# Expert weight chunks fetched as two 1 MB transfers instead of one of 2 MB

## The chip, the cores and the metric

The kernel runs on one core of one Trainium2 chip. The metric is the time of one execution on the device in microseconds (us). TensorE (PE) does the matrix products, VectorE (DVE), ScalarE (ACT) and GpSimd (POOL) do the rest, and SyncE (SP) issues all DMA transfers.

## The reference

One inference step of a two-layer backbone for 128 prompt tokens and 256 sample tokens, all in float32, with a model width of 1024. Each layer has four parallel token mixers with gates (half one) and then an expert-choice feed-forward stage (half two). The change touches the second half:

```python
def expert_choice_ffn(h, w_router, w_gate, w_up, w_down):
    B, L, D = h.shape
    cap = EC_CAPACITY * L // N_EXPERTS          # 16 prompt, 32 sample tokens per expert
    aff = jax.nn.softmax((h @ w_router).astype(jnp.float32), axis=-1)
    g, idx = lax.top_k(jnp.swapaxes(aff, 1, 2), cap)
    xs = jax.vmap(lambda hb, ib: hb[ib])(h, idx)
    a = jnp.einsum('becd,edf->becf', xs, w_gate)
    u = jnp.einsum('becd,edf->becf', xs, w_up)
    y = jnp.einsum('becf,efd->becd', jax.nn.silu(a) * u, w_down) * g[..., None].astype(h.dtype)
    return jax.vmap(lambda ib, yb: jnp.zeros((L, D), yb.dtype).at[ib.reshape(-1)].add(yb.reshape(-1, D)))(idx, y)
```

There are 16 experts. Each has three 1024x1024 float32 matrices (gate, up, down), 12 MB, so that a layer's experts are 192 MB (201 million bytes) which are read once.

## The kernel before, in words

**Chunks.** An expert's weights lie in memory as six chunks of 2 MB: four (PAIRS = 4) of gate and up, each for two of the eight blocks k of the contraction, and two of down, each for four blocks k. A chunk is 128 rows, one for a partition, of 16 KB: four sub-rows of 1024 words. A gate/up block k needs two sub-rows (gate, up), a down block k one. PER = 6 chunks make an expert and 96 make a layer; below they are counted as x = 0 to 95.

**The ring.** Eight places hold chunks (RING = 8, order in PLACE): six are slots of the array `ring`, one is `high_slot`, and one is made of two pieces, `low_slot` for three sub-rows and a stretch of the constants' array C for the fourth (place 7, with x = 1, 9, 17, ...). `fetch` issues a chunk as one DMA (lines 565, 566 and 568: place 7 takes two, of 1.5 and 0.5 MB), all from SP on one queue. `chunk_landed` is PE's wait on the semaphore e_land of the place.

**Order on SP.** `mixer_sync` issues x = 0 to 6 before the expert stage, as places come free from the mixers' use of the same memory; its first four go out early, x = 4 to 6 when the output projection has ended. `experts_sync` issues x = 7, and then waits for each chunk n to be used up (`used_chunk`) before it issues x = n + 8 into its place. Chunk use is told by PE: e_pair after the second block k of the first three gate/up chunks, the closing of the product's PSUM bank after the fourth, e_down_half after k = 3 of down, and the closing of y after k = 7. After the last chunk SP issues the next layer's small parameters (line 747), the four modulation chunks ada0 to ada3 (line 727) and the first input weights in two transfers of 1 MB (line 733, rows of 8 KB).

**Order on PE.** `experts_tensor` loops over groups of four experts. For each it does `gate_up` (line 1702, with the gathers of line 1670 between the blocks of the first expert of a group), then `down`: transposes (lines 1716 and 1719) and products (line 1731). In the trace a float32 product counts as two MATMUL records. A group ends with idle products (line 692) and the combination (line 1748). After the last group of layer 0 PE goes on to the opening of layer 1 (lines 698, 635, 638 and 639); line 900, DVE's line 1367 and line 934 then begin its mixers.

```python
if k % 2 == 0:
    chunk_landed(pe, g, j * PER + k // 2)
...
if k % 2 and k < KT - 1:
    ins.then_inc(S["e_pair"], 1)
```

Of the kernel before, what the change touches and what calls it, by code (L numbers as in the profile page):

```python
# [29 lines left out]
D = 1024  # L30
KT = D // P
# [108 lines left out]
def build(nc, A):  # L140
    ctx = ExitStack()
    with ctx:
# [5 lines left out]
        def sem(name):  # L148
            s = ctx.enter_context(nc.semaphore(name))
            sems.append(s)  # L150
            return s
# [69 lines left out]
        def adas(c):  # L221
# [94 lines left out]
        names = ("x_mixed b_high b_rest br_high br_rest rest_in grow_in sink_in cache_in nab_in nab_ready u_zero "  # L316
                 "sc_ready dve_step route_step conv_step rope_ready scores_done scores_read nmax_ready exps_done p_ready "
                 "pv0 pv1 high_act rest_pool high_dve rest_dve w_high w_rest mask_in dft_in gate_add out_kv n2_sq n2_ms n2_sd n2_rs n2_xn wr_in wrm_ready router_max router_exp wk_prompt aff_ready affg_ready "
                 "cum_ready sel_ready selg_ready e_pair e_down_half silu_done x_done prompt_part").split() + list(OPENING)
        land = [sem(f"land{s}") for s in range(NSLOT)]  # L320
        e_land = [sem(f"e_land{s}") for s in range(8)]
        full = [sem(f"full{b}") for b in range(8)]
        free = [sem(f"free{b}") for b in range(8)]
        e_full = [sem(f"e_full{b}") for b in range(8)]
# [5 lines left out]
            scores_read=6, nmax_ready=6, exps_done=7, p_ready=6, pv0=6, pv1=6, high_act=4, rest_pool=4, high_dve=4,  # L330
            rest_dve=4, w_high=48, w_rest=48, mask_in=16, dft_in=16, gate_add=24, out_kv=64, n2_sq=4, n2_ms=3, n2_sd=3,
            n2_rs=3, n2_xn=3, wr_in=16, wrm_ready=2, router_max=1, router_exp=1, wk_prompt=2, aff_ready=1, affg_ready=1,
            cum_ready=1, sel_ready=5, selg_ready=5, e_pair=48, e_down_half=16, silu_done=32, x_done=12, prompt_part=8, op_full=3, op_free=2,
            op_prm=1, op_mod=2, op_gain=1, op_sq=3, op_sd=3, op_rs=3, op_xn=3)
        assert set(PER_LAYER) == set(names)

# [137 lines left out]
        def layer(l):  # L474
# [77 lines left out]
            PER = PAIRS + 2  # L552
            PLACE = (4, 7, 6, 5, 1, 2, 0, 3)
            RING = len(PLACE)

            def chunk(l, e, i):

                name, part = ("w_e_gu", i) if i < PAIRS else ("w_e_down", i - PAIRS)
                return A[name][bass.ds(l, 1), bass.ds(e, 1), part].rearrange("o e p n -> p (o e n)")

            def fetch(sp, x, src):

                s, landing = PLACE[x % RING], e_land[x % RING]
                if s == 7:
                    sp.dma_start(low_slot, src[:, 0:3 * D]).then_inc(landing, 16)
                    sp.dma_start(C[:, FIRST:FIRST + D], src[:, 3 * D:4 * D]).then_inc(landing, 16)
                else:
                    sp.dma_start(high_slot if s == 6 else ring[:, s, :], src).then_inc(landing, 16)

            def chunk_row(x, r):  # L570

# [2 lines left out]
                    return low_slot[:, r * D:(r + 1) * D] if r < 3 else C[:, FIRST:FIRST + D]  # L574
                return (high_slot if s == 6 else ring[:, s, :])[:, r * D:(r + 1) * D]

            def chunk_landed(pe, g, x):

                n = 32 if PLACE[x % RING] == 7 else 16
                pe.wait_ge(e_land[x % RING], n * (l * NE * PER // RING + x // RING + 1) + g * (n * GRP * PER // RING))  # L580


            E = BankTurns()
# [203 lines left out]
            def mixer_sync(sp):  # L787
# [50 lines left out]

                for x in range(RING - 1):
                    s = PLACE[x]  # L840
                    if s < 4:
                        used_up(sp, latest[s])
                    elif s == 4:
                        copied(sp, f"o{len(ATT) - 1}")
                    elif s == 5:
                        take(sp, f"p{GATE_ORDER[-1]}_{KT - 1}")
                    elif s == 6:
                        sp.wait_ge(S["gate_add"], base("gate_add") + 3 * KT)
                    elif s == 7:
                        take(sp, parts[-1][0])  # L850
                    fetch(sp, x, chunk(l, x // PER, x % PER))

            def mixer_gpsimd(pool):
                pool.wait_ge(S["op_full"], base("op_full") + 1)
# [740 lines left out]


            def experts_sync(sp):
                def used_chunk(g, j, i):

                    if i < PAIRS - 1:  # L1600
                        sp.wait_ge(S["e_pair"], base("e_pair") + (PAIRS - 1) * (GRP * g + j) + i + 1)
                    elif i == PAIRS - 1:
                        e_take(sp, g, f"gu{j}_1")
                    elif i == PAIRS:
                        sp.wait_ge(S["e_down_half"], base("e_down_half") + GRP * g + j + 1)
                    else:
                        e_take(sp, g, f"y{j}")

                if l > DEPTH - 2:
                    sp.wait_ge(S["x_mixed"], base("x_mixed") + 2 * TT)  # L1610
                    sp.dma_start(GROW[:, 0, 0, :], A["final_norm_g"].rearrange("(o d) -> o d", o=1).broadcast_to((P, D))).then_inc(
                        once["fin_g_in"], 16)
                used_up(sp, "ada11")
                fetch(sp, RING - 1, chunk(l, (RING - 1) // PER, (RING - 1) % PER))
                with sp.Fori(0, NE // GRP - 1) as g:
                    for n in range(GRP * PER):
                        used_chunk(g, n // PER, n % PER)
                        x = n + RING
                        fetch(sp, x, chunk(l, g * GRP + x // PER, x % PER))
                last = NE // GRP - 1  # L1620
                for n in range(GRP * PER - RING):
                    used_chunk(last, n // PER, n % PER)
                    x = n + RING
                    fetch(sp, x, chunk(l, last * GRP + x // PER, x % PER))

                if l < DEPTH - 1:
                    load_parameters(sp, l + 1)
                    for name in ("ada0", "ada2", "ada1", "ada3", "w0"):
                        n = GRP * PER - RING + PLACE.index(unit_at[name][0])
                        used_chunk(last, n // PER, n % PER)  # L1630
                        if name == "w0":
                            load_first_weights(sp, l + 1)
                        else:
                            load_ada(sp, l + 1, int(name[3:]))

                if l > DEPTH - 2:
                    for i, t in enumerate(ROWS):
                        dst = A["y_prompt"] if t == 0 else A["y_sample"][:, (t - 1) * P:t * P]
                        sp.wait_ge(once["fin_y"], i + 1)
                        sp.dma_start(dst.rearrange("b s d -> (b s) d"), XN[:, t, :]).then_inc(once["fin_out"], 16)  # L1640
                    sp.wait_ge(once["fin_out"], TT * 16)

            def experts_tensor(pe):
# [20 lines left out]
                with pe.Fori(0, NE // GRP) as g:  # L1664
# [21 lines left out]
                    def gate_up(j):  # L1686

                        pb = [e_open(pe, g, f"gu{j}_{half}") for half in range(2)]
                        for k, halves in [(k, (0, 1)) for k in range(KT - 2)] + [(k, (half,)) for half in range(2) for k in (KT - 2, KT - 1)]:
                            if j == 0 and 0 in halves and 0 < k < KT - 1:  # L1690
                                for ahead in ((k + 1,) if k < KT - 3 else (k + 1, k + 2) if k == KT - 3 else ()):
                                    gather(ahead)
                                if k == KT - 2:
                                    affinities_t()
                            if k % 2 == 0:
                                chunk_landed(pe, g, j * PER + k // 2)
                            if j == 0 and 0 in halves:
                                e_copied(pe, g, f"xe{k}")
                            for half in halves:
                                for m in range(2):  # L1700
                                    w = chunk_row(j * PER + k // 2, 2 * (k % 2) + m)
                                    ins = nc.tensor.matmul(pb[half][64 * m:64 * m + 64, :], XE[:, k, j, :],  # L1702
                                                           w[:, half * CH:(half + 1) * CH], start=(k == 0),
                                                           stop=(k == KT - 1))
                                if k == KT - 1:
                                    e_close(ins, f"gu{j}_{half}")
                            if k % 2 and k < KT - 1:
                                ins.then_inc(S["e_pair"], 1)

                    def down(j):  # L1710
                        for k in range(KT):
# [12 lines left out]
                        for k in range(KT):  # L1724
                            if k % 4 == 0:
                                e_copied(pe, g, f"at{j}_{k // 4}")
                            x = j * PER + PAIRS + k // 4
                            if k % 4 == 0:
                                chunk_landed(pe, g, x)
                            for half in range(2):  # L1730
                                ins = nc.tensor.matmul(ps[64 * half:64 * half + 64, :], AT[:, k, :],  # L1731
                                                       chunk_row(x, k % 4)[:, half * CH:(half + 1) * CH],
                                                       start=(k == 0), stop=(k == KT - 1))
                            if k == 3:
                                ins.then_inc(S["e_down_half"], 1)
                        e_close(ins, f"y{j}")

                    for j in range(GRP):
# [277 lines left out]
```

## Time and profile before

| | us |
|---|---|
| three runs | 1712.97, 1716.68, 1717.48; median 1716.68 |
| the profiled execution | 1710.48, with a span of 1708.4 |
| PE busy | 1578.7 (92% of the span) |
| DVE, ACT, POOL busy | 505.0, 489.6, 322.2 |
| q1, SP's DMA queue | 52296 packets, 535.43 MB, 76.4% of 16 engines' span |

The DMA engines are busy in nine tenths and more of every slice from some 430 us to the end of the first expert stage (850 us), and again from some 1260 to 1685 us. In these stretches they move 427 to 429 GB/s. The granted clock of TensorE is at full speed in nearly all slices.

### The profile page before, as it was taken

What the parts mean: (1) busy time and instruction counts of PE and PEld (TensorE: products, weight loads), DVE (VectorE), ACT (ScalarE), POOL (GpSimd) and SP (SyncE); (2) the same over time, 40 slices, a digit from 0 to 9 for tenths busy, and PEclk for the clock granted to TensorE, in tenths of its full rate; (3) what the DMA queues carried; (4) which work ended last, traced back from release to release, by engine and by line L of the source; (5) the groups of instructions that cost most, each with busy time, mean ns of one, the idle gap of its engine ahead of it and who ended that gap; (6) DMA issues with size and microseconds to landing.
All of it is one profiled execution on the core that took longest, in us unless ns stands there. A gap on an engine that the chain in (4) does not pass through costs nothing.

```text
span 1708.4 us, 20755 instructions
## 1 busy us (share of the span) xinstructions
PE 1578.7 (92%) x8277; PEld 936.1 (55%) x8277; DVE 505.0 (30%) x854; ACT 489.6 (29%) x892; POOL 322.2 (19%) x182
## 2 busy tenths in 40 slices
PE   7999999999999899799899999999999998988986
PEld 4988899944333333243269888897533432432422
DVE  3723454423120121121157234533321211112113
ACT  4435454214012121120153455431321211211211
POOL 1544456400000000000035444552000000000000
PEclk9999999999999999999999999999999999999999
DMA  9624433558999999999994433356499999999995
GB/s 382 227 99 157 149 148 148 196 248 322 423 427 427 428 428 427 429 427 427 423 394 155 140 117 148 148 185 251 183 399 428 427 428 427 427 428 427 428 428 244
DMA packets 52357, 536.29 MB, mean 314 GB/s; under 512 B 13616, under 2 KB 14024, under 8 KB 20296
## 3 DMA queue, kind: packets, MB, share of 16 engines
q1 hardware_dynamic: 52296, 535.43, 76.4%
q8 instruction: 43, 0.70, 0.2%
q14 instruction: 18, 0.15, 0.0%
HBM read 533.05 MB, written 2.36 MB: 313 GB/s over the span
## 4 chain that ended last, share of the span: by engine, by line
PE 70%; DMA 21%; DVE 4%; ACT 3%; issue 1%; SPq 0%; POOL 0%; DVEq 0%; ACTq 0%
PE psum L934 22%; PE psum L1702 18%; DMA ring<-in_w_e_down 12%; PE psum L1731 8%; DMA ring<-in_w_e_gu 7%; PE psum L1167 4%; PE psum L1097 3%; PE psum L1670 3%; PE psum L698 2%; PE psum L1748 2%; DMA ring<-in_w_ada 1%; PE psum L692 1%; PE psum L1070 1%; PE psum L1049 1%; ACT WSR L1186 1%
## 5 line engine op out<-in xcount | busy, mean ns | idle before, releaser
L934 PE MATMUL psum<-HTH,WSR 128*128 128x384 f32 x1536 | 411.4, 341 | 4.8 <-DVE HTL L1378 4.2
L1702 PE MATMUL psum<-ring,arena 128*64 128x512 f32 x1536 | 344.7, 596 | 36.5 <-DMA ring<-in_w_e_gu 34.6
L934 PEld LDWEIGHTS psum<-HTH,WSR 128*128 128x128 f32 x1536 | 279.4, 188 | 18.4 <-issue 11.4
L878 POOL TENSOR_TENSOR WSR<-ring,WSR 128x1024 fp32r<-128x1024 f32 x94 | 228.9, 2435 | 255.2 <-ACT WSR L1186 255.2
L934 PE MATMUL psum<-HTL,WSR 128*128 128x384 f32 x768 | 258.7, 337 | 0.0
L1702 PEld LDWEIGHTS psum<-ring,arena 128*64 128x64 f32 x1536 | 105.4, 137 | 255.5 <-issue 189.0
L1879 DVE TENSOR_TENSOR arena<-arena,psum 64x512 f32<-64x512 f32 x64 | 44.1, 690 | 507.4 <-ACT arena L1785 507.4
L1186 ACT ACTIVATE WSR<-ring 128x1024 fp32r<-128x1024 f32 x96 | 101.6, 1058 | 289.1 <-PE psum L934 289.1
L1731 PE MATMUL psum<-ring,arena 128*64 128x512 f32 x768 | 172.8, 596 | 3.7 <-DMA ring<-in_w_e_down 3.7
L934 PEld LDWEIGHTS psum<-HTL,WSR 128*128 128x128 f32 x768 | 144.3, 188 | 1.0 <-issue 1.0
L1785 ACT ACTIVATE arena<-psum 64x512 f32<-64x512 f32 x64 | 37.7, 589 | 347.3 <-PE psum L1702 346.6
L1702 PE MATMUL psum<-arena 128*64 128x512 f32 x448 | 119.8, 599 | 8.0 <-DMA arena<-in_w_e_gu 8.0
L1790 ACT ACTIVATE arena<-psum 32x512 f32<-32x512 f32 x64 | 37.7, 590 | 269.2 <-PE psum L1731 268.8
L1731 PEld LDWEIGHTS psum<-ring,arena 128*64 128x64 f32 x768 | 53.7, 137 | 102.0 <-issue 100.4
L1868 DVE TENSOR_TENSOR arena<-psum,GROW 32x512 f32<-32x512 f32 x64 | 43.8, 684 | 210.4 <-PE psum L1731 210.0
L855 POOL MEMSET arena<- 128x888 f32 x2 | 1.7, 837 | 545.4 <-PE psum L698 545.4
L620 ACT ACTIVATE arena<-psum,MOD,SC 128x128 f32<-128x128 f32 (+1 forms) x144 | 57.2, 460 | 123.2 <-PE psum L1670 118.7
L1167 PE MATMUL psum<-ring,arena 128*128 128x512 f32 x192 | 85.4, 596 | 3.1 <-DMA ring<-in_w_out 1.6
L1468 DVE TENSOR_TENSOR arena<-arena 128x384 f32<-128x384 f32 x48 | 72.2, 1503 | 1.7
L1702 PEld LDWEIGHTS psum<-arena 128*64 128x64 f32 x448 | 34.2, 136 | 67.4 <-issue 63.5
L1670 PEld LDWEIGHTS psum<-arena,XN 128*128 128x128 f32 x384 | 47.0, 191 | 37.5 <-issue 37.5
L1465 DVE TENSOR_TENSOR arena<-arena,psum 128x384 f32<-128x384 f32 x48 | 26.6, 554 | 130.5 <-ACT arena L1279 111.8
(218 smaller groups left out, 1622.8 us busy)
## 6 DMA issues: line engine op xcount, KB each, us to landing
ring<-in_w_e_gu SPq DMA_DIRECT2D x96, 2048.0 KB, 28.1
ring<-in_w_e_down SPq DMA_DIRECT2D x48, 2048.0 KB, 31.0
ring<-in_w_ada SPq DMA_DIRECT2D x24, 2048.0 KB, 9.4
ring<-in_w_in SPq DMA_DIRECT2D x22, 2048.0 KB, 8.2
arena<-in_w_e_gu SPq DMA_DIRECT2D x16, 2048.0 KB, 30.0
arena<-in_w_e_gu SPq DMA_DIRECT2D x16, 1536.0 KB, 23.6
arena<-in_w_e_down SPq DMA_DIRECT2D x8, 2048.0 KB, 23.4
arena<-in_w_e_down SPq DMA_DIRECT2D x8, 1536.0 KB, 28.6
```

The costliest lines, as they stand in the source:

```text
L620: return nc.scalar.activation(dst, src, ACT.Identity, scale=SC[:, which, k, i:i + 1], bias=MOD[:, sec * KT + k, i:i + 1])
L878: nc.gpsimd.tensor_tensor(WSR[:, 1, i % 2], part_src(i), WSR[:, 0, i % 2].bitcast(F32), ALU.subtract).then_inc(S["w_rest"], 1)
L934: ins = nc.tensor.matmul(ps[:, 0:TOK], WSR[:, w, i % 2, k, :], x[:, k, :], start=(k == 0 and w == 0 and x is HTH), stop=(k == KT - 1 and w ...
L1097: ins = nc.tensor.matmul(ps[:, 0:TOK], w[:, idx % 2, c, :], x[:, c, :], start=(ins is None), stop=(c == 1 and w is BWL))
L1167: ins = nc.tensor.matmul(ps[:, :], MRG[:, k, t * P:(t + 1) * P], wo[:, k % 4, half * CH:(half + 1) * CH], start=(k == 0), stop=(k == KT - 1))
L1186: nc.scalar.activation(WSR[:, 0, i % 2], part_src(i), ACT.Copy).then_inc(S["w_high"], 1)
L1468: nc.vector.tensor_tensor(MRG[:, k, :], MRG[:, k, :], GP[:, idx % 2, :], ALU.add).then_inc(S["gate_add"], 1)
L1670: ins = nc.tensor.matmul(ps[:, c0:c0 + P], XN[:, t, k * P:(k + 1) * P], SEL[:, AT_PLACE[t]].rearrange("p e s -> p (e s)"), start=(t != 2), ...
L1702: ins = nc.tensor.matmul(pb[half][64 * m:64 * m + 64, :], XE[:, k, j, :], w[:, half * CH:(half + 1) * CH], start=(k == 0), stop=(k == KT - 1))
L1731: ins = nc.tensor.matmul(ps[64 * half:64 * half + 64, :], AT[:, k, :], chunk_row(x, k % 4)[:, half * CH:(half + 1) * CH], start=(k == 0), ...
L1868: ins = nc.vector.tensor_tensor(YS[rows, cols], ps[64 * half:64 * half + 32, :], GROW[64 * half:64 * half + 32, 1, 1, cols], ALU.mult)
L1879: e_release(nc.vector.tensor_tensor(AA[0:64, cols], TMP[64:128, cols], ps[64:128, :], ALU.mult), f"gu{j}_{half}")
```

## The change

Every chunk goes as two transfers, one of sub-rows 0 and 1 and one of sub-rows 2 and 3; rows of 16 KB in the transfer become rows of 8 KB. Each half has its own landing semaphore (16 in place of 8). PE waits for the half that a block needs, and says that it has used a half; SP waits for a half and then issues the half that takes its memory. Place 7 now takes three transfers: 1 MB, 0.5 MB and 0.5 MB. The number of bytes, the ring, the order of the chunks and PE's products stay as they are.

```diff
-            def fetch(sp, x, src):
-                s, landing = PLACE[x % RING], e_land[x % RING]
-                if s == 7:
-                    sp.dma_start(low_slot, src[:, 0:3 * D]).then_inc(landing, 16)
+            def fetch(sp, x, h, src):
+                s, landing = PLACE[x % RING], e_land[x % RING][h]
+                if s == 7 and h:
+                    sp.dma_start(low_slot[:, 2 * D:3 * D], src[:, 2 * D:3 * D]).then_inc(landing, 16)
                     sp.dma_start(C[:, FIRST:FIRST + D], src[:, 3 * D:4 * D]).then_inc(landing, 16)
                 else:
-                    sp.dma_start(high_slot if s == 6 else ring[:, s, :], src).then_inc(landing, 16)
+                    rows = slice(2 * h * D, 2 * (h + 1) * D)
+                    dst = low_slot if s == 7 else high_slot if s == 6 else ring[:, s, :]
+                    sp.dma_start(dst[:, rows], src[:, rows]).then_inc(landing, 16)
...
-                def used_chunk(g, j, i):
-                    if i < PAIRS - 1:
-                        sp.wait_ge(S["e_pair"], base("e_pair") + (PAIRS - 1) * (GRP * g + j) + i + 1)
-                    elif i == PAIRS - 1:
-                        e_take(sp, g, f"gu{j}_1")
-                    elif i == PAIRS:
-                        sp.wait_ge(S["e_down_half"], base("e_down_half") + GRP * g + j + 1)
+                def used_half(g, j, i, h):
+                    done = base("e_half") + HALVES * (GRP * g + j)
+                    if i < PAIRS:
+                        if (i, h) == (PAIRS - 1, 1):
+                            e_take(sp, g, f"gu{j}_1")
+                        else:
+                            sp.wait_ge(S["e_half"], done + 2 * i + h + 1)
+                    elif (i, h) == (PER - 1, 1):
+                        e_take(sp, g, f"y{j}")
                     else:
-                        e_take(sp, g, f"y{j}")
+                        sp.wait_ge(S["e_half"], done + KT - 1 + 2 * (i - PAIRS) + h + 1)
...
                     for n in range(GRP * PER):
-                        used_chunk(g, n // PER, n % PER)
                         x = n + RING
-                        fetch(sp, x, chunk(l, g * GRP + x // PER, x % PER))
+                        for h in range(2):
+                            used_half(g, n // PER, n % PER, h)
+                            fetch(sp, x, h, chunk(l, g * GRP + x // PER, x % PER))
...
-                            if k % 2 == 0:
-                                chunk_landed(pe, g, j * PER + k // 2)
+                            if k < KT - 2 or 0 in halves:
+                                chunk_landed(pe, g, j * PER + k // 2, k % 2)
...
-                            if k % 2 and k < KT - 1:
-                                ins.then_inc(S["e_pair"], 1)
+                            if k < KT - 1 and 1 in halves:
+                                ins.then_inc(S["e_half"], 1)
...
-                            if k % 4 == 0:
-                                chunk_landed(pe, g, x)
+                            if k % 2 == 0:
+                                chunk_landed(pe, g, x, k % 4 // 2)
...
-                            if k == 3:
-                                ins.then_inc(S["e_down_half"], 1)
+                            if k % 2 and k < KT - 1:
+                                ins.then_inc(S["e_half"], 1)
```

## Rows read from the trace of the kernel before

**Rows 1.** The DMA queues' view of 450 to 845 us: packets, MB, share of 16 engines.
```profile
DMA packets 13038, 168.92 MB, mean 428 GB/s; under 512 B 1448, under 2 KB 1448, under 8 KB 2728
q1 hardware_dynamic: 13036, 168.89, 100.7%
```
**Rows 2.** PE's waits of 1300 to 1700 us: total us, times, longest us.
```profile
PE psum L1702 <- DMA ring<-in_w_e_gu: 17.3, 15, 1.2
PE psum L1702 <- DMA arena<-in_w_e_gu: 4.0, 3, 1.4
```
**Rows 3.** Chain that ended last, its end: start us, us, what.
```profile
1653.13 35.45 DMA ring<-in_w_e_down
1688.59 0.14 issue
1688.72 3.65 PE psum L1731 x16
1692.38 1.49 PE psum L692 x4
```
**Rows 4.** SP's DMA issues at the first stage's start: start us, us of issuing.
```profile
389.88 0.81 SPq L568 DMA_DIRECT2D ring<-in_w_e_down  x2
410.89 0.36 SPq L568 DMA_DIRECT2D ring<-in_w_e_gu  x1
415.95 0.34 SPq L565 DMA_DIRECT2D arena<-in_w_e_gu  x1
422.06 0.33 SPq L568 DMA_DIRECT2D arena<-in_w_e_down  x1
426.13 0.33 SPq L568 DMA_DIRECT2D ring<-in_w_e_down  x1
```
**Rows 5.** The chain of waits in the same stretch: PE's first blocks k.
```profile
405.62 1.94 PE psum L1702 x8
407.55 0.87 PE psum L1670 x6
408.42 1.87 PE psum L1702 x8
```
**Rows 6.** Stretches of 10 us, both stages' starts: busy us (instructions), then clock, DMA share, GB/s.
```profile
410.00:420.00 10.00, 10.00 (x58) 5.16 (x56) 0.00 (x0) 3.04 (x8) 0.00 (x0) 1.00 0.90 338
420.00:430.00 10.00, 9.04 (x48) 3.54 (x49) 1.80 (x3) 4.23 (x8) 0.00 (x0) 1.00 0.98 371
430.00:440.00 10.00, 10.00 (x48) 3.30 (x46) 1.36 (x2) 1.19 (x2) 0.00 (x0) 1.00 0.98 406
1250.00:1260.00 10.00, 10.00 (x58) 5.08 (x58) 0.00 (x0) 3.61 (x10) 0.00 (x0) 1.00 0.98 394
1260.00:1270.00 10.00, 9.05 (x49) 3.40 (x46) 1.80 (x3) 3.66 (x6) 0.00 (x0) 1.00 0.97 363
```
**Rows 7.** DMA queues of 464 to 496 us: rows of 16 KB nearly alone.
```profile
DMA packets 995, 13.78 MB, mean 431 GB/s; under 512 B 109, under 2 KB 109, under 8 KB 169
q1 hardware_dynamic: 994, 13.76, 101.2%
```
**Rows 8.** DMA queues of 866 to 871 us: the first input weights, rows of 8 KB.
```profile
DMA packets 247, 2.05 MB, mean 410 GB/s; under 512 B 30, under 2 KB 30, under 8 KB 30
q1 hardware_dynamic: 247, 2.05, 97.7%
```
**Rows 9.** SP's issues before the first stage ends.
```profile
815.39 16.09 SPq L747 DMA_DIRECT2D arena<-in_conv_ln_g  x1
842.67 2.36 SPq L727 DMA_DIRECT2D ring<-in_w_ada  x1
```
**Rows 10.** Line 727's last issue, 842 to 846 us: time from issue to landing.
```profile
DMA to landing us min/median/max: 26.6/26.6/26.6
```
**Rows 11.** The chain of waits at the first stage's end.
```profile
849.33 3.65 PE psum L1731 x16
867.78 4.85 PE psum L698 x32
872.63 1.88 PE psum L900 x16
```
**Rows 12.** PE's weight loads of line 698, in order of time.
```profile
868.63 0.20 PEld L698 LDWEIGHTS psum<-ring,condT 128*32 128x32 f32 x4 [0.65 <-issue]
870.31 0.12 PEld L698 LDWEIGHTS psum<-ring,condT 128*32 128x32 f32 x4 [0.63 <-issue]
```

More of the change, by code:

```diff
@@ L318, in build @@
                  "pv0 pv1 high_act rest_pool high_dve rest_dve w_high w_rest mask_in dft_in gate_add out_kv n2_sq n2_ms n2_sd n2_rs n2_xn wr_in wrm_ready router_max router_exp wk_prompt aff_ready affg_ready "
-                 "cum_ready sel_ready selg_ready e_pair e_down_half silu_done x_done prompt_part").split() + list(OPENING)
+                 "cum_ready sel_ready selg_ready e_half silu_done x_done prompt_part").split() + list(OPENING)
         land = [sem(f"land{s}") for s in range(NSLOT)]
-        e_land = [sem(f"e_land{s}") for s in range(8)]
+        e_land = [[sem(f"e_land{s}_{h}") for h in range(2)] for s in range(8)]
         full = [sem(f"full{b}") for b in range(8)]
@@ L332, in build @@
             n2_rs=3, n2_xn=3, wr_in=16, wrm_ready=2, router_max=1, router_exp=1, wk_prompt=2, aff_ready=1, affg_ready=1,
-            cum_ready=1, sel_ready=5, selg_ready=5, e_pair=48, e_down_half=16, silu_done=32, x_done=12, prompt_part=8, op_full=3, op_free=2,
+            cum_ready=1, sel_ready=5, selg_ready=5, e_half=160, silu_done=32, x_done=12, prompt_part=8, op_full=3, op_free=2,
             op_prm=1, op_mod=2, op_gain=1, op_sq=3, op_sd=3, op_rs=3, op_xn=3)
@@ L554, in layer @@
             RING = len(PLACE)
+            HALVES = KT - 1 + KT // 2 - 1
             def chunk(l, e, i):
@@ L575, in chunk_row, with chunk_landed @@
                 return (high_slot if s == 6 else ring[:, s, :])[:, r * D:(r + 1) * D]
-            def chunk_landed(pe, g, x):
-                n = 32 if PLACE[x % RING] == 7 else 16
-                pe.wait_ge(e_land[x % RING], n * (l * NE * PER // RING + x // RING + 1) + g * (n * GRP * PER // RING))
+            def chunk_landed(pe, g, x, h):
+                n = 32 if PLACE[x % RING] == 7 and h else 16
+                pe.wait_ge(e_land[x % RING][h], n * (l * NE * PER // RING + x // RING + 1) + g * (n * GRP * PER // RING))
             E = BankTurns()
@@ L850, in mixer_sync @@
                         take(sp, parts[-1][0])
-                    fetch(sp, x, chunk(l, x // PER, x % PER))
+                    for h in range(2):
+                        fetch(sp, x, h, chunk(l, x // PER, x % PER))
             def mixer_gpsimd(pool):
@@ L1613, in experts_sync @@
                 used_up(sp, "ada11")
-                fetch(sp, RING - 1, chunk(l, (RING - 1) // PER, (RING - 1) % PER))
+                for h in range(2):
+                    fetch(sp, RING - 1, h, chunk(l, (RING - 1) // PER, (RING - 1) % PER))
                 with sp.Fori(0, NE // GRP - 1) as g:
                     for n in range(GRP * PER):
-                        used_chunk(g, n // PER, n % PER)
                         x = n + RING
-                        fetch(sp, x, chunk(l, g * GRP + x // PER, x % PER))
+                        for h in range(2):
+                            used_half(g, n // PER, n % PER, h)
+                            fetch(sp, x, h, chunk(l, g * GRP + x // PER, x % PER))
                 last = NE // GRP - 1
                 for n in range(GRP * PER - RING):
-                    used_chunk(last, n // PER, n % PER)
                     x = n + RING
-                    fetch(sp, x, chunk(l, last * GRP + x // PER, x % PER))
+                    for h in range(2):
+                        used_half(last, n // PER, n % PER, h)
+                        fetch(sp, x, h, chunk(l, last * GRP + x // PER, x % PER))
                 if l < DEPTH - 1:
@@ L1629, in experts_sync @@
                         n = GRP * PER - RING + PLACE.index(unit_at[name][0])
-                        used_chunk(last, n // PER, n % PER)
+                        used_half(last, n // PER, n % PER, 1)
                         if name == "w0":
```

## The prediction

> **What bounds the kernel now.** I read the slices first, then the DMA queues of one long stretch, PE's waits, and last the chain's end. From 450 to 845 us the engines of the queue are busy for 100.7% of their time, and they move 168.92 MB in 395 us, which is 427.6 GB/s [rows 1]. The second expert stage looks the same. A stretch with full queues can't be shortened by earlier waits or earlier issues: its end is the moment at which the queue last ran empty, plus the bytes left by the rate. PE looks busy, but it is the one that waits: some 18 stalls of at most 1.4 us on gate and up chunks in the second stage [rows 2]. So three things can move the time here: what the queue loses before it is full, what each transfer costs in it, and what PE still has to do when the last transfer has landed. One chunk is 2.097 MB, 4.90 us at 427.6 GB/s.
>
> The chain ends with such a tail. The last down chunk, issued at 1653.13, lands 35.45 us later, and behind it PE needs 3.65 us for 16 records, then 1.49 us of idle products and the combination [rows 3].
>
> **Part 1, the fill: a gain of 3.5 and 2.4 us.** At 389.88 us the queue is started for good with x = 4 [rows 4]. Chunks 4 to 7 occupy it until about 411. x = 8 is issued at 410.89, when PE has used up both blocks of chunk 0, so it can't be in time; x = 9, 10 and 11 follow at 415.95, 422.06 and 426.13 [rows 4], 5.1, 6.1 and 4.1 us apart against 4.90 us of transfer. Here the queue is served as it comes, with a gap ahead of many transfers. The stretches show it: 338, 371 and 406 GB/s in three times 10 us [rows 6], which is (3 x 427.6 - 1115) x 10 / 427.6 = 3.9 us lost. In the second layer two of them run at 394 and 363 [rows 6], 2.3 us lost, with some tenths in their neighbours; I take 2.6.
>
> With halves, the first half of chunk 0 is given back after block k = 0, which ends at 407.55, where the second ends at 408.42 + 1.87 = 410.29 [rows 5]. That is 2.7 us earlier, before the queue is empty, and the 2.45 us of that half cover the next return at 410.89. The same holds for each of the next, at the same 2.73 us for a block: half x = 9 at some 413.7 behind a queue that has work to 416.8, x = 10 at 419.1 with work to 421.8. So I expect the queue not to run empty again after x = 4. I take 3.5 of the 3.9 us in layer 0 and 2.4 of 2.6 in layer 1, the rest for window edges and slow first packets. The ends are 0 (the loss has another cause than gaps) and the whole.
>
> **Part 2, twice as many rows: a loss of 6.0 us in each layer.** A row of 16 KB is one packet, and a chunk is 8 of them on each of 16 engines; in the change it is 16 of 8 KB. If a packet has a cost of its own, the full queue pays it. In 32 us with little but 16 KB rows, 994 packets take 101.2% of 16 x 32 us = 518.1 us [rows 7]. 109 are completion packets (under 512 B), 60 have 4 KB, 825 have 16 KB. From 4 KB to 16 KB I need one more size, and the first input weights have it [rows 8]: 247 packets, 30 of them completions, take 0.977 x 80 = 78.2 us for 2.05 MB. That mix is 33 of 16 KB and 184 of 8 KB. With 616 ns for 16 KB (518.1 less 60 x 0.16, by 825), 8 KB come to (78.2 - 33 x 0.616) / 184 = 314 ns. Two of them are 629, 12 ns over one of 16 KB. Part of it is overlap and not time: over 395 us the packets' sum is 0.7% more than 16 engines have [rows 1], 44 us on 11,588 data packets, 3.8 ns each. That leaves 8 ns, and by eight packets 0.065 us for a chunk, the additional completion packet in it. The upper end is 12.3 ns by eight, 0.10 us. The lower end is 0, since 4 KB rows of place 7 in the same stretch leave no dip that I can see in 427.6. I take 0.065, the value that the packet rows give; over x = 4 to 95, 92 chunks, 6.0 us for a layer.
>
> The Trainium skill has a rule against this change, in "DMA: Bandwidth & Descriptors", section Bandwidth: batch transfers to at least 1 MiB for 75% of the peak, with 341 GB/s measured at 1 MB. By it each chunk would take 2.097 / 0.341 = 6.15 us, and the sum would be 1.25 x 92 x 2 = 230 us more. Place 7 already goes as 1.5 and 0.5 MB in the stream that averages 427.6 GB/s [rows 1], so the trace speaks against the rule wherever transfers queue behind each other.
>
> **Part 3, SP.** Each issue takes 0.33 us [rows 4], so a half costs SP well under the 2.45 us that it occupies the engines. A queue can be full: one issue of a few rows took 16.09 us, near the stage's end with all the last chunks ahead of it [rows 9]. With twice the packets SP will stand longer in such issues. Behind it waits only SP's own next transfer, and a full queue is what the engines need; I count nothing. If the held issue let the queue run dry it would cost what the gaps of part 1 cost, 3 to 4 us.
>
> **Part 4, PE.** More waits and increments (per expert 5 more waits, 6 more increments) lie beside 1.2 us of waiting in each chunk (4.90 less 3.65). In the first group of experts PE is ahead of nothing but its own fill, and there the stock of eight chunks covers tenths. Nothing, with up to 1 us as the other end.
>
> **Part 5, the tail: a gain of 1.8 us in the second layer.** Of the 16 records after the last landing, 8 belong to the first half, which lands 2.45 us earlier and needs 1.83. So 1.83 us go from the path [rows 3]. In layer 0 the same 1.83 us come before the combination [rows 11], but there is a second path to the layer's opening: the stream behind the experts. The last of the ada chunks was issued at 842.67 and landed 26.6 us later, at 869.3 [rows 9, 10], and PE's line 698 is at work on the second pair from 867.78, with its last loads from 870.31 on [rows 11, 12]. The first input weights come right behind. That is a slack of about 1 us.
>
> **The sum.** Layer 0: the stream ends 6.0 - 3.5 = 2.5 us later; the products' path is 2.5 - 1.8 = 0.7 later, the path over the ada chunks 2.5 less 1 of slack = 1.5 later. The later one counts: +1.5. Layer 1: 6.0 - 2.4 = 3.6 later, less 1.8 of tail: +1.8. Together +3.3 us. On the profiled execution's 1710.5 that is 1713.8; the median of the runs is 6.2 us above that execution, so I put it on the median: 1720. This is 0.19%, and 0.3% (5.1 us) is about what a measurement of this kernel can tell from no change.
>
> **The rivals.** (A) The toll of the smaller rows is the full 0.10 us for a chunk (the overlap doesn't help, or memory reads in 8 KB pieces are slower than the first input weights show). Then 9.2 us go in each layer: layer 0 +5.7 less 1 of slack, layer 1 +6.8 - 1.8, together +9.7, 1726. Its place is every chunk behind x = 4, and it decides from 0.075 us on, where the sum passes 5.1. For it: 12 ns are what the rows give undiscounted. Against: the packets' sum exceeds the time that there is. (B) No toll: what I took for a cost per packet is how starts and ends are recorded. Then layer 0 has -3.5 (the ada path), layer 1 -2.4 - 1.8, together -7.7, 1709. It needs a toll under 0.02 us, and the two sizes' rows then have to be wrong by 10 ns. (C) The change does not do what it says in the fill: the halves come early, but the low rate from 410 to 440 is the engines' start and not gaps. Then +3.5 and +2.4 are back in, +9.2, 1726. Against it: the rate falls again and again as long as issues come one by one, and never after. (D) A transfer of 1 MB runs slower as such, the page's case: +230 us, 1947.
>
> **How the numbers follow.** Forecast with tolls of 0.03 to 0.075 us 0.58; A 0.18; C 0.08; B 0.14; D 0.02. The forecast's cases lie between -1 and +5 us, 1716 to 1722. A and C reach 1726, B 1709; the range 1711 to 1727 leaves out the far part of B, and D. Slower by over 0.3%: all of A, C and D, and 0.02 of the forecast's edge: 0.30. Faster: 0.13, most of B. Same: 0.57.
>
> **What would show it.** Packets on SP's queue rise from 52296 by some 24,600 data packets and 3,000 completions. From 450 to 845 us the rate falls from 427.6 to about 422 GB/s (by 1.3%): at 427 it is B, below 420 A. The three stretches after 410 us show over 415 GB/s: if not, C. The last wait of PE on a transfer is followed by 8 records in 1.8 us. I am wrong altogether if the queue shows gaps between 450 and 845 us, or if SP's held issues are followed by an idle queue.

## The result, and the profile after

The changed kernel takes 1720.09 us (median of 11 runs, 1717.09 to 1722.06) against 1714.32 (11 runs) before: ratio 1.0033, 95% interval 1.0025 to 1.0042, so 5.7 us slower. The forecast time was 1720.0, and that it was met is partly luck: it stood 3.3 us over a median of three runs that lay 2.4 us higher than that of eleven, and the size of the change was short by the same 2.4 us. The parts below say where.

| | before | after |
|---|---|---|
| median us | 1714.32 | 1720.09 |
| the profiled execution, its span | 1710.48, 1708.4 | 1718.99, 1716.9 |
| packets on q1 | 52296 | 79944 |
| granted clock, mean | 0.997 | 0.991 |

The DMA queues of the changed kernel from 450 to 845 us, to be set beside [rows 1]:

```profile
DMA packets 24271, 166.28 MB, mean 421 GB/s; under 512 B 2697, under 2 KB 2697, under 8 KB 5257
q1 hardware_dynamic: 24268, 166.23, 101.4%
```

The engines are as busy as before and move 2.64 MB less in 395 us: 421.0 GB/s for 427.6. Eight chunks, one turn of the ring (16.78 MB), take 39.85 us for 39.23. That is 0.077 us for a chunk, and 7.1 us over 92 chunks of a layer: the toll of the change in a full queue.

The fill, that is the time until the queue is full, in stretches of 10 us (busy us of the engines, then clock, DMA share, GB/s), to be set beside [rows 6]; the second stage begins 5.87 us later than before:

```profile
410.00:420.00 10.00, 10.00 (x58) 5.30 (x58) 0.00 (x0) 3.18 (x9) 0.00 (x0) 1.00 1.00 406
420.00:430.00 10.00, 9.04 (x47) 3.39 (x45) 1.80 (x3) 4.07 (x8) 0.00 (x0) 1.00 1.01 405
430.00:440.00 10.00, 10.00 (x50) 3.41 (x48) 1.36 (x2) 1.18 (x2) 0.00 (x0) 1.00 0.98 380
...
1250.00:1260.00 10.00, 9.77 (x53) 4.52 (x53) 1.94 (x4) 3.90 (x10) 0.00 (x0) 1.00 1.01 405
1260.00:1270.00 10.00, 10.00 (x55) 4.50 (x53) 0.00 (x0) 4.53 (x10) 0.00 (x0) 1.00 1.02 423
```

Against its own 421 the first stage loses (1263 - 1191) x 10 / 421 = 1.7 us where it lost 3.9, the second 0.4 where it lost 2.6. The gain is 2.2 us in each, in this execution.

The end of the chain that ended last, to be set beside [rows 3]:

```profile
1663.96 25.02 DMA ring<-in_w_e_gu
1688.98 0.04 issue
1689.02 2.82 PE psum L1711 x12
...
1691.87 0.60 ACT arena L1794
...
1692.49 0.70 DVE arena L1888
...
1693.91 7.02 PE psum L1740 x32
1700.93 1.49 PE psum L695 x4
```

The last down chunk is no longer waited for. From the last gate/up half on, PE, ScalarE, VectorE and all 32 down records stand in a row, 11.95 us. The last down half landed under it: it was issued at 1671.51 and took 27.4 us, so it was there at 1698.9, and 8 records behind it would have ended at the same 1700.9. The end of the products moved from 1692.37 [rows 3] to 1700.93, by 8.56 us, of which the later start of the stage has 5.87 and the stage itself 2.7. The first issues of SP in the second stages, of the kernel before and then of the changed one, give that start:

```profile
1229.30 0.80 SPq L568 DMA_DIRECT2D ring<-in_w_e_down  x2
```

```profile
1235.17 0.80 SPq L571 DMA_DIRECT2D ring<-in_w_e_down  x2
```

At the end of the first stage PE looks like this in the changed kernel (start us, us; in brackets the idle time ahead and what ended it):

```profile
838.26 1.94 PE L1711 MATMUL psum<-ring,arena 128*64 128x512 f32 x8 [0.56 <-DMA ring<-in_w_e_gu]
840.75 1.08 PE L1711 MATMUL psum<-ring,arena 128*64 128x512 f32 x4 [0.56 <-DMA ring<-in_w_e_gu]
843.23 4.49 PE L1711 MATMUL psum<-ring,arena 128*64 128x512 f32 x12 [1.40 <-DMA ring<-in_w_e_gu]
...
849.75 7.09 PE L1740 MATMUL psum<-ring,arena 128*64 128x512 f32 x32
```

Down to 840.75 each half brings 8 records and is followed by some 0.56 us of idleness. The fourth gate/up chunk is worked through by output halves (blocks 6 and 7 for the first, then for the second), so its first half brings only 4 records, and a wait of 1.40 us comes behind. Then the same 12 records take 4.49 us that took 2.8 in layer 1 (above). The clock says why:

```profile
840.00:844.00 4.00, 2.04 (x8) 0.41 (x8) 0.00 (x0) 0.00 (x0) 0.00 (x0) 0.92 1.02 424
844.00:848.00 4.00, 4.00 (x16) 1.31 (x13) 0.69 (x1) 0.81 (x2) 0.00 (x0) 0.65 1.00 418
```

In the change the granted clock falls from 2.4 to the lower of its two levels, 1.2 GHz, for a short time. It makes the products end 1.7 us later. They end at 856.84 for 852.98 [rows 11], with the stage's first issue at 389.71 for 389.88 [rows 4]: 4.0 us for this stage.

Not all of the 1.7 us is lost. The opening of layer 1 also waits for the last ada chunk, which was issued at 847.77 and took 25.4 us, so it landed at 873.2. Its 16 records of 1.92 us could have been done at 485.4 us after the stage's first issue; the opening's next line, 904, began at 876.48, which is 486.8. So the clock's fall cost at most 1.3 us here. Before, line 900 began at 872.63 [rows 11], 482.8 us after the first issue.

The wait of 1.40 us alone does not bring the clock down. The two stages have ten waits of 1.39 to 1.41 us ahead of 12 records, and behind five of them (at 604, 724, 843, 1540 and 1659 us) the 12 records take 4.5 us; behind the other five it stays at its upper level.

### The profile page after: what moved, and what is told of

The parts are those of the page before. It is cut to its first block, busy times and chain, and to the rows that moved or that the text cites. A ratio compares the mean times of both kernels' runs of the same rounds, so it can differ in the third digit from the quotient of the medians.

```text
span 1716.9 us, 21415 instructions
## 1 busy us (share of the span) xinstructions
PE 1594.0 (93%) x8277; PEld 936.7 (55%) x8277; DVE 504.8 (29%) x854; ACT 489.2 (28%) x892; POOL 322.2 (19%) x182
## 3 DMA queue, kind: packets, MB, share of 16 engines
q1 hardware_dynamic: 79944, 535.45, 77.1%
## 4 chain that ended last, share of the span: by engine, by line
PE 67%; DMA 12%; SPq 11%; DVE 4%; ACT 3%; issue 2%; POOL 0%; DVEq 0%; ACTq 0%
PE psum L938 22%; PE psum L1711 16%; DMA ring<-in_w_e_gu 10%; SPq L571 9%; PE psum L1740 8%; PE psum L1171 4%; PE psum L1101 3%; PE psum L701 2%; PE psum L1679 2%; PE psum L1757 2%; DMA ring<-in_w_ada 1%; SPq L566 1%; PE psum L695 1%; PE psum L1074 1%; DVE arena L1888 1%
## 5 line engine op out<-in xcount | busy, mean ns | idle before, releaser
L1711 PE MATMUL psum<-ring,arena 128*64 128x512 f32 x1536 | 359.6, 610 | 41.6 <-DMA ring<-in_w_e_gu 39.5
L1740 PE MATMUL psum<-ring,arena 128*64 128x512 f32 x768 | 171.4, 595 | 0.0
```

## The experiments

**Two transfers without the gains.** PE waits for both halves and SP issues both when the chunk is used up.

```diff
+                        used_half(g, n // PER, n % PER, 1)
                         for h in range(2):
-                            used_half(g, n // PER, n % PER, h)
                             fetch(sp, x, h, chunk(l, g * GRP + x // PER, x % PER))
...
```

> Each chunk still goes as two transfers of 1 MB with rows of 8 KB, but PE waits for both before the first block of the chunk and SP issues both when the whole chunk is used: the toll without the gains. Theory T (toll of the smaller rows on a full queue, 0.076 us for a chunk as the ring's turn shows after the change, over 92 chunks in each layer): 7.0 us in each layer, less 1 us of slack in layer 0, so +12 to +14 us over the kernel before. Rival C (the loss is TensorE's clock, which fell to half speed several times in the trace after the change when PE waited for halves): with whole waits those falls go, 0 to +2 us.

1725.69 us (6 runs), ratio 1.0078 (1.0066 to 1.0090), +13.4 us. The toll is there at its full size once fill and tail are given up, and the clock is at 0.996 to 0.997. T holds; the clock can't be the main part. (The C of this expectation is the clock, not the prediction's C.)

**Small rows, one transfer.** The weights of a chunk lie as two blocks [128, 2048], and one DMA takes both.

```diff
-                    sp.dma_start(high_slot if s == 6 else ring[:, s, :], src).then_inc(landing, 16)
+                    dst = high_slot if s == 6 else ring[:, s, :]
+                    sp.dma_start(dst.rearrange("p (h n) -> p h n", h=2), src).then_inc(landing, 16)
...
```

> One transfer of 2 MB for a chunk as before the change, one wait and one return, but its rows are cut in two of 8 KB each by another order of the weights in memory (place 7: 8, 4 and 4 KB). The number of packets is that of the change, the number of transfers that of before. Theory T1 (the toll belongs to the packet): the turn of the ring is 39.7 to 39.9 us and the time +11 to +14 us. Rival T2 (it belongs to the transfer, its completion packets and its issue): turn 39.2 to 39.3 us, time within 1.5 us of before.

1724.64 us (6 runs), ratio 1.0074 (1.0059 to 1.0088), +12.7 us. Its DMA queues from 450 to 845 us:

```profile
DMA packets 23173, 166.33 MB, mean 421 GB/s; under 512 B 1592, under 2 KB 1592, under 8 KB 4152
```

The completion packets (under 512 B) are back from 2697 to 1592, and the rate stays down. The toll belongs to the data packet; the second transfer with its completions and its issue adds what separates this run from the one before, some 0.7 us of 13, which is within their intervals.

**Two transfers, one for 64 partitions each**, rows of 16 KB.

```diff
-                    sp.dma_start(high_slot if s == 6 else ring[:, s, :], src).then_inc(landing, 16)
+                    dst = high_slot if s == 6 else ring[:, s, :]
+                    for h in range(2):
+                        sp.dma_start(dst[64 * h:64 * h + 64, :], src[64 * h:64 * h + 64, :]).then_inc(landing, 16)
...
```

> Each chunk goes as two transfers of 1 MB, one for 64 partitions and one for the other 64, so rows stay at 16 KB (place 7 as before); both are waited for and issued together. The number of transfers is that of the change, that of data packets is that of before. T1 (packet): +0 to +2 us, the 16 more completion packets of some 9 ns on 16 engines alone. T2 (transfer): +11 to +14 us. If a transfer over 64 partitions does not spread over the engines evenly, the rate in the full stretch shows it below 420 GB/s.

2570.5 us (6 runs), ratio 1.5055 (1.4999 to 1.5112). As a test of T1 against T2 it failed, since something larger covers it. Its queues from 600 to 1000 us:

```profile
DMA packets 7546, 90.47 MB, mean 226 GB/s; under 512 B 1383, under 2 KB 1383, under 8 KB 2025
q1 hardware_dynamic: 7546, 90.47, 100.8%
```

The engines are fully busy and move half. 5521 packets of 16 KB or, for place 7, 12 KB take some 1.15 us each (6451 us less 0.16, an estimate, for each of 642 of 4 KB); the same mix took some 0.60 before ([rows 1]: 6364 us for 10,308 such packets and 1280 of 4 KB). The Trainium skill ("DMA: Bandwidth & Descriptors", section The descriptor swizzle) has partitions 0 to 63 on the even ports and 64 to 127 on the odd ones; by that a transfer over 64 partitions has half the ports. The halved rate agrees, but no run here shows the ports, and why the rate is halved stays open.

**Whole chunks under PE's split waits.** As the change on PE; SP issues whole chunks and raises the second semaphore itself.

```diff
+            def fetch_whole(sp, x, src):
...
+                    sp.dma_start(high_slot if s == 6 else ring[:, s, :], src).then_inc(landing[0], 16)
+                sp.sem_inc(landing[1], 16)
...
```

> PE's waits and returns stand by halves as in the change, with their semaphores, but every chunk is one transfer of 2 MB again (SP raises the second semaphore itself) and is issued when it is wholly used. Theory T: nothing is split on the queue, so no toll, and whole chunks land, so no gains: within 1.5 us of before. Rival C (more waits and increments in PE's stream cost time, or bring the clock down): +3 to +6 us, with falls of the granted clock in the expert stages of its profile.

1714.27 us (11 runs), ratio 1.0003 (0.9994 to 1.0012): no difference. PE's additional waits and increments cost nothing that these runs can tell. The clock does fall in its trace, twice in the second stage, each time behind a wait of 2.1 us for a chunk of place 7 (before, such waits were at most 1.4 us [rows 2]; the stages have six of 2.1 us):

```profile
1431.14 5.35 PE L1727 MATMUL psum<-arena 128*64 128x512 f32 x16 [2.09 <-DMA arena<-in_w_e_gu]
```

These 16 records took 3.65 us elsewhere, yet the stage is as long as before to 0.4 us (463.5 for 463.1): inside a stage whose queue is full, these falls hid. The same kernel is the base for the next three, in which single chunks x of each layer go by halves.

**Fill, tail, and both.** The diff is one line on that base; this is the one for both, the fill has x = 8 to 15 alone and the tail x = 93 to 95:

```diff
-            HALVED = ()
+            HALVED = (8, 9, 10, 11, 12, 13, 14, 15, 93, 94, 95)
```

> Only x = 8 to 15 of each layer go by halves. T: the loss of 3.9 and 2.6 us between the first issue and the full queue shrinks to 1.7 and 0.4 us (as in the trace after the change), toll 8 x 0.076 x 2 = 1.2 us: -3 to -4 us. F: +1 us.

1711.81 us (12 runs), ratio 0.9988 (0.9978 to 0.9998), -2.1 us, with an interval of -3.8 to -0.3. It is short of the -3 to -4 that T expected, though the interval doesn't exclude it; F's +1 is out. The trace says where it falls short:

```profile
420.00:430.00 10.00, 9.04 (x53) 4.42 (x53) 1.72 (x3) 4.84 (x9) 0.00 (x0) 1.00 1.03 352
430.00:440.00 10.00, 10.00 (x50) 3.40 (x48) 1.45 (x3) 1.18 (x2) 0.00 (x0) 1.00 0.97 392
```

The kernel without halves runs in these two stretches at 373 and 390 GB/s. So in layer 0 a part of the low rate is no gap between issues: the engines are busy (shares 1.03 and 0.97) and slow, and halves don't lift it. Over the three stretches from 410 us the two kernels differ by 0.9 us in layer 0.

> Only x = 93 to 95 of each layer go by halves. T: the last landing stays where it is (toll 0.2 us), and 8 records in place of 16 follow it: -1.6 us in layer 1; in layer 0 the products end 1.6 us earlier, of which the ada chunks' landing lets through up to 1 us. -1.5 to -2.6 us in all. Rival: the chain from the last gate/up half over ACT, DVE and the transposes is as long, and the gain is 0 to -0.7 us.

1711.63 us (12 runs), ratio 0.9985 (0.9975 to 0.9995), -2.6 us (-4.3 to -0.9), as T has it.

> Only x = 8 to 15 (those that refill the ring first) and x = 93 to 95 (the last gate/up and both down chunks) go by halves in each layer; the other 85 chunks are single transfers of 2 MB. Theory T (fill and tail gains are real, the toll is the packets'): toll 11 x 0.076 x 2 = 1.7 us; fill -2 to -3 us in each layer; tail -1.6 us in each layer, in layer 0 bounded by the stream to the ada chunks with 1 us of slack. Together -4 to -7 us against before, 1707 to 1710. Rival F (no gain in the fill, the low rate there is the engines' start): -1 to 0 us.

1708.47 us (6 runs), ratio 0.9966 (0.9952 to 0.9979): 5.8 us under before and some 11 under the change, the best version found. It keeps the 16 KB rows for 85 of 96 chunks. Its chain at the end (start us, us, what):

```profile
1643.47 35.56 DMA ring<-in_w_e_gu
1679.03 0.04 issue
1679.07 2.82 PE psum L1727 x12
...
1683.96 7.02 PE psum L1756 x32
```

It is the chain of the changed kernel, 11.95 us from the last gate/up half to the end of the products, 10 us earlier in time.

**Contiguous halves.** Each half is one MB in a row in memory.

```diff
-                    sp.dma_start(dst[:, rows], src[:, rows]).then_inc(landing, 16)
+                    sp.dma_start(dst[:, rows], src[:, h, :]).then_inc(landing, 16)
...
```

> The change, but each half is one contiguous MB in HBM (before it is 128 pieces of 8 KB at a pitch of 16 KB). Theory T: the toll is of the packet, whatever lies where: within 1.5 us of the changed kernel, +5 to +7 us over before, ring's turn 39.8 us. Rival M (reading 8 KB out of every 16 KB is what costs): turn back to 39.3 us and the time 4 to 8 us under before, since the gains of fill and tail stay.

1719.87 us (6 runs), ratio 1.0030 (1.0014 to 1.0046), +5.1 us, the change's own time; 166.29 MB from 450 to 845 us, the change's own rate. Where the 8 KB lie does not matter; M is out.

**The order in the last gate/up chunk.** On the change:

```diff
-                        for k, halves in [(k, (0, 1)) for k in range(KT - 2)] + [(k, (half,)) for half in range(2) for k in (KT - 2, KT - 1)]:
+                        for k, halves in [(k, (0, 1)) for k in range(KT)]:
```

> The change, with the last gate/up chunk of each expert worked through block by block (k = 6 for both output halves, then k = 7), so that 8 records wait on each half and the wait of 1.40 us in the middle of the chunk goes; the product of the first output half closes later, so ScalarE's and VectorE's part starts up to 0.9 us later. Theory K (the falls of TensorE's clock that were seen behind these waits cost the change 1 to 2 us where they hit a stage's end): no clock falls in the profile's full stretches, and 1 to 2 us under the changed kernel, +3.5 to +4.5 us over before. Rival (the falls lie in time that the DMA stream covers, or the later closing takes back what they cost): within 1 us of the changed kernel, +5 to +7 us over before.

1718.13 us (12 runs), ratio 1.0026 (1.0016 to 1.0035), +4.5 us. PE's waits from 1300 to 1700 us, of the changed kernel and then of this one (total us, times, longest us):

```profile
PE psum L1711 <- DMA ring<-in_w_e_gu: 21.0, 32, 1.4
```

```profile
PE psum L1711 <- DMA ring<-in_w_e_gu: 17.0, 32, 0.6
```

The long wait is gone, and so are the clock's falls in both stages; here are 840 to 848 us:

```profile
840.00:844.00 4.00, 3.43 (x16) 0.77 (x12) 0.00 (x0) 0.00 (x0) 0.00 (x0) 1.00 1.00 418
844.00:848.00 4.00, 2.57 (x14) 1.04 (x14) 1.38 (x2) 1.37 (x3) 0.00 (x0) 1.00 1.02 426
```

Over all runs the mean clock is 0.995 to 0.999 here, and 0.989 to 0.998 in the change. So the falls go when the long waits go, as K has it. Its price is not shown, since 4.5 and 5.7 us have overlapping intervals (2.7 to 6.0 and 4.3 to 7.2). Its chain also ends as I had forecast it for the change, with 8 records behind the last landing:

```profile
1670.79 27.31 DMA ring<-in_w_e_down
1698.10 0.04 issue
1698.14 1.94 PE psum L1740 x8
```

**The stages one by one.** From a stage's first issue on SP (x = 4) to the end of its products, in each profiled execution, in us:

| kernel | layer 0 | layer 1 |
|---|---|---|
| before | 463.1 | 463.1 |
| the change | 467.1 | 465.8 |
| two transfers, no gains | 469.9 | 469.9 |
| small rows, one transfer | 469.1 | 469.1 |
| whole chunks | 463.4 | 463.5 |
| fill | 463.5 | 462.1 |
| tail | 461.3 | 462.7 |
| fill and tail | 460.9 | 460.6 |
| contiguous halves | 466.8 | 467.2 |
| order | 465.7 | 465.5 |

The toll stands here without the noise of the rest: 6.8 us in each stage with two transfers, 6.0 with one. The fill brings 1.4 to 2 us in layer 1, but at most 0.5 in layer 0, net of its own toll. The kernel with contiguous halves has the clock's fall at the end of layer 1 (12 records in 4.47 us) and none at the end of layer 0. These are single executions, and the same stretch differs by about 1 us between them: in layer 0 the last gate/up half lands 453.5 us after the first issue in the change and 454.5 with contiguous halves, at the same rate.

## Why the prediction was right, and which terms were off

The direction and the mechanism held: a toll on every chunk in a full queue, against a gain in the fill and one at the tail. The time was met more closely than the parts deserve, and that is luck: the toll came out 2.2 us larger and the fill 1.5 us smaller than forecast, and the median that it was put on was 2.4 us too high.

- **Part 1, fill.** The gaps close (share 1.00 and 1.01 up to 430 us), but the gain is 2.2 and 2.2 us where I took 3.5 and 2.4. The mis-sized term is layer 0's. I had put every lost tenth down to gaps between issues; but from 430 to 440 us the engines are busy (0.98) and slow whatever is split: 406 GB/s before, 380 in the change (1.0 us of its 1.7), 390 to 392 in the kernels of the fill experiment. What that dip is stays open. My mark of over 415 GB/s in all three stretches was missed. C, that the low rate is no gap, is true for this part of it, and not for the rest.
- **Part 2, toll.** 0.077 us for a chunk, where I took 0.065 between 0 and 0.10; 7.1 us in a layer for 6.0. The deduction for overlap was too large: 12.3 ns by eight packets was 0.10, and the truth lies between. It is past the 0.075 us from which I had let A begin. (The stages above give 0.074 with two transfers and 0.065 with one, on the other side of that mark.) As a mechanism A is the same one; I put the boundary inside my own uncertainty. B is excluded by the small rows; its sum had a slip besides, since by the rule of the sum its layer 0 is -3.5 less 1 of slack, and B would have been 1708. D is excluded by 1 MB transfers that run at 421 GB/s; a half is still the 1 MiB that the rule quoted there asks for, so that rule does not speak against the change.
- **Part 3, SP.** Its issues are held, as said: two of them from 486.75 us on take 6.57 us, and 11% of the chain is SP's. It costs nothing that the trace shows, since the rate is even, and small rows in half as many transfers are nearly as slow as two transfers (+12.7 and +13.4 us).
- **Part 4, PE.** The waits as such are free. What I had not seen is that a half of the fourth gate/up chunk brings only 4 records, which makes the long wait, and that the clock falls behind some of these waits.
- **Part 5, tail.** 1.8 us was right as a bound of the stream, and the order experiment shows those 8 records, in 1.94 us. In the change another chain is as long: the last half of gate/up, 12 records, ScalarE, VectorE, transposes and all of down. The two are level, so the size held. In layer 0 the path that I had named, over the ada chunks, is the later one where the clock doesn't fall: in the order experiment the last ada chunk, issued at 846.50, landed 28.0 us later, and line 904 began at 876.55, behind 16 records from 874.63 on.

```profile
874.63 1.92 PE psum L701 x16
876.55 1.88 PE psum L904 x16
```

That is 485.5 us after the stage's first issue for 482.8 before, +2.7. In the profiled execution of the change the clock's fall made the products' path later still, +4.0.
- **The sum.** With the measured terms layer 1 is 7.1 - 2.2 - 1.8 = 3.1 us later. In layer 0 the products' path gives the same 3.1, but the path over the ada chunks 7.1 - 2.2 - 1.0 of slack = 3.9, and by the prediction's own rule the later one counts: 7.0 together. With the 2.7 us of the order experiment for layer 0 it is 5.8. The runs say 5.7 (4.3 to 7.2). The profiled execution is 8.5 us longer: 4.0 and 2.7 in the stages, and 1.8 outside them. This last part is not shown to be the change's: from line 904 (900, 914) to the second stage's first issue the executions take 356.6 to 358.7 us, the kernel before 356.7, the change 358.7, and the tail kernel 358.7 too.

## What to carry to other kernels

Where a DMA queue is full for hundreds of microseconds, look first at what each byte costs in it: rows of 16 KB cut into 8 KB cost 1.5% of the rate, more than all earlier starts gave back. Split transfers only where the queue runs dry (when it is refilled) and where somebody waits for the last one; 11 of 96 chunks by halves gave -0.34%, all of them +0.33%. Read gains and tolls from the stretches in which each works, and let a term's whole interval fall into one case.

## What the runs showed of the hardware that was not expected

- Rows of 8 KB in place of 16 KB (128 partitions, queue full): 421.0 for 427.6 GB/s, with one transfer or two, and contiguous in memory or not.
- A transfer over 64 partitions with rows of 16 KB: 226 GB/s with the engines 100.8% busy, against 428 over 128 partitions.
- TensorE's clock fell to its lower level (1.2 GHz) behind waits of 1.40 us in stretches in which PE had worked 8 records and idled 0.56 us by turns: behind 5 of 10 such waits in the change, 3 of 10 with contiguous halves, and 2 of 6 waits of 2.1 us with whole chunks. Without such waits, in the order experiment, it did not fall in a stage, nor before, with 16 records and waits of at most 1.4 us by turns [rows 2].
- A fall of the clock inside a stage whose queue is full made 16 records 1.7 us longer (5.35 for 3.65) and left the stage as long as before to 0.4 us.
